# A recurrent mixer whose state step becomes one whole-array product, with its states kept and its output products in two batches

## The chip, the cores and the metric

The kernel runs on one core of a Trainium2 chip. The metric is the device time of one execution in microseconds (us). Three runs of the kernel before gave 2497.30, 2500.01 and 2503.43 us, so the median is 2500.01 us.

A core has engines that run side by side and wait for one another through semaphores: TensorE (PE; its weight loads are listed as PEld), VectorE (DVE), ScalarE (ACT), GpSimd (POOL) and SyncE (SP), which here only issues DMAs. PE writes into PSUM, eight banks of 128 partitions by 512 float32. All data here is float32. The trace records each float32 matmul as two MATMUL records with their weight loads, so its counts are twice those of the code.

## What is computed

One decoder layer over 1024 tokens of width 1024. Its first mixer, the one changed, is a recurrence with 16 heads of 64 channels:

```
S = S * w_t + (S a_t) b_t + v_t k_t        per head, S is 64 x 64
y_t = S r_t
y = (y - mean) / sqrt(var + eps) * w + b + bonus, then times a gate
```

The kernel does not step by token. It cuts the tokens into 16 chunks of 64, and for each chunk works out, by products that need no state, a transition E, an additive term L, a read-out matrix R and a local output Yl. What stays sequential is, for c = 0 to 15 and each head,

```
S(c+1) = E(c) S(c) + L(c)                  the chain
Y(c)   = S(c) R(c) + Yl(c)                 the outputs (each up to transposition)
```

## The kernel before

All work on this mixer is in phase_rwkv. Eight passes p = 0 to 7 (PAIRS) handle two heads each, head h on partitions 64h to 64h+63. Each engine has its own program in the code, written out by hand in the order of issue. In each pass PE makes the masked products of the chunks (grams) and transposes (turn), then the projections for pass p+1 (paired, project_v), then two stages chunks(p, g) with g = 0 and 1, of eight chunks each.

A stage on PE is, in order: X4 (level, for g = 0; for g = 1 it was made during the stage before), T4/N4 (L949, L952), X5 (L961), N5 (L972), UT (L986), ER (L994, which gives E and R), LY (L1008, which gives L and Yl), and then the chain of eight steps. Most of these are products of 64x64 matrices on quarters of the array. Each needs a VectorE or ScalarE result of the one before, and to hide that wait the code puts pieces of an unrelated projection between them: side(n) issues n products of 128x128 weights with 512 columns, and gap(p, g, i) is side(4). 28 such products make one unit of that projection, in the order M2, M1, M6, M7, M4, M5, M3. early(p, g) is true for g = 1 and p at most 5; such a stage holds 32 of them, the last four already of the next unit, the others 24 or 28.

A chain step on PE (L1016 to L1036) waits for the state, makes E(c) S(c) as one 64x64 product for each head (L1023), then the output product S(c) R(c), again one for each head (L1027), and in g = 0 on every second step four products of X4 for the next stage (L901). A side product follows on every second step, or on every step if early. VectorE adds L(c) to the result and writes the state into Sf, two buffers of 64 columns used in turn (L1682). After the last step VectorE adds Yl to all outputs of the stage into Y (L1691).

VectorE's stage (chunks at L1624) is also in a fixed order. For g = 1 it is: the mask of X4 (L1636), two steps of the generator beside (between(2), here the products at L1508 and L1512 for pass p+1), four sums of projection weights (side_sums, L1422 to L1430), and then the two additions into TN (L1643) for which PE's X5 waits. Later it fills ET with the decay on the diagonal (L1666) and adds E (L1672). GpSimd makes sums of projection weights and clears TN (L1373).

## Time and profile before

| | |
|---|---|
| median of three runs | 2500.01 us |
| span of the profiled execution | 2496.2 us |
| PE busy, share of the span | 2412.2 us, 97% |
| DVE busy | 1243.1 us, 50% |
| ACT busy | 570.2 us, 23% |
| POOL busy | 99.8 us, 4% |
| the eight passes lie at | about 145 to 1176 us |
| one pass lasts | about 129 us |

A time of a row is counted from the span's start. The start-to-start distance of two rows of PE is how long the engine was held by the first; the duration of a single matmul is longer, because matmuls are pipelined. An entry in brackets is the idle time of the engine ahead of the row and what ended it. PEclk is the clock that TensorE was granted, 1.00 for 2.4 GHz and 0.50 for 1.2 GHz.

### The profile page before, as it was taken

The numbers are of one execution on the slowest core, as the hardware profiler recorded it, in microseconds if no ns is written. First come the engines' busy times: TensorE is split into PE (matmuls) and PEld (weight loads), VectorE is DVE, ScalarE is ACT, GpSimd is POOL, SyncE is SP. The second block draws the span as 40 slices with busy tenths as digits, with TensorE's granted clock in tenths as the row PEclk, the third lists the DMA queues.
The fourth block names the chain that finished last, engine by engine and source line by source line (L and its number), as shares of the span: only waits on it lengthen the run. The fifth ranks groups of instructions, "written<-read, shape, count | busy, mean of one in ns | idle before, by whom it ended". The sixth has DMA issues, their size and how long they took to land. (4 is left out here: it accounts for less than half of the span.)

```text
span 2496.2 us, 39012 instructions
## 1 busy us (share of the span) xinstructions
PE 2412.2 (97%) x16519; PEld 1288.4 (52%) x16519; DVE 1243.1 (50%) x2080; ACT 570.2 (23%) x949; POOL 99.8 (4%) x97
## 2 busy tenths in 40 slices
PE   9999999999999999989999999999999999999996
PEld 5644557454565454744445976644455444443342
DVE  4646676767675858563585634465444411101103
ACT  3322323223232424121111354411100000000002
POOL 1000000000000000000000000000000100000002
PEclk9999999999999999999999999999999999999998
DMA  4111212121212121122434823163263999999997
GB/s 155 40 49 38 70 49 70 45 70 49 70 45 64 38 79 35 61 65 73 161 76 127 302 97 102 39 208 109 74 220 133 413 428 428 427 427 424 428 428 294
DMA packets 214908, 406.18 MB, mean 163 GB/s; under 512 B 64979, under 2 KB 166861, under 8 KB 202445
## 3 DMA queue, kind: packets, MB, share of 16 engines
q1 hardware_dynamic: 187152, 336.42, 36.9%
q10 hardware_dynamic: 22108, 47.32, 5.2%
q0 software_dynamic: 5472, 19.93, 2.1%
q8 instruction: 132, 2.16, 0.4%
q14 instruction: 44, 0.35, 0.0%
HBM read 329.07 MB, written 68.26 MB: 159 GB/s over the span
## 5 line engine op out<-in xcount | busy, mean ns | idle before, releaser
L3317 PE MATMUL moe_pp<-moe_ring,own_xT 128*128 128x512 f32 (+1 forms) x624 | 235.5, 599 | 1.4 <-DVE own_xT L3072 1.4
L3175 DVE COPY own_hidT<-moe_pp 128x512 f32<-128x512 f32 x22 | 15.2, 691 | 270.9 <-PE moe_pp L3326 270.9
L3317 PEld LDWEIGHTS moe_pp<-moe_ring,own_xT 128*128 128x128 f32 (+1 forms) x624 | 89.7, 167 | 107.0 <-issue 105.0
L742 PE MATMUL rwkv_pp<-mix_hT,rwkv_side_raw 128*128 128x512 f32 x240 | 116.7, 621 | 8.0 <-DMA rwkv_side_raw<-w_in 4.1
L3340 PE MATMUL moe_pp<-moe_ring,own_hidT 128*64 128x512 f32 (+1 forms) x368 | 120.1, 594 | 0.8 <-DVE own_hidT L3175 0.8
L2881 PE MATMUL moe_pp<-moe_ring,mix_hT 128*128 128x512 f32 x256 | 117.5, 610 | 3.3 <-DVEq L179 3.3
L671 PE MATMUL rwkv_pp<-mix_hT,rwkv_wt_kv 128*128 128x512 f32 x256 | 113.3, 595 | 0.0
L742 PE MATMUL rwkv_pp<-rwkv_TS,rwkv_side_sum 128*128 128x512 f32 x240 | 109.9, 601 | 2.8 <-ACT rwkv_TT L1259 1.7
L742 PE MATMUL rwkv_pp<-rwkv_TS,rwkv_side_raw 128*128 128x512 f32 x240 | 110.6, 603 | 0.8
L1682 DVE TENSOR_TENSOR rwkv_Sf<-rwkv_pp,rwkv_LY 128x64 f32<-128x64 f32 x128 | 28.7, 225 | 161.0 <-PE rwkv_pp L1023 161.0
L2309 PE MATMUL attn_pp<-att_yC,attn_wp 128*128 128x512 f32 x224 | 100.7, 597 | 0.0
L3436 ACT ACTIVATE own_yo<-moe_pp 128x1024 f32<-128x1024 f32 x22 | 22.5, 1024 | 324.7 <-PE moe_pp L3340 324.7
L1188 ACT ACTIVATE rwkv_side_zx<-rwkv_pp 128x512 f32<-128x512 f32 x40 | 23.9, 597 | 271.4 <-PE rwkv_pp L742 200.2
L3181 DVE TENSOR_TENSOR own_hid<-moe_pp,own_act_h 128x512 f32<-128x512 f32 x22 | 15.2, 692 | 139.1 <-PE moe_pp L3317 139.1
L3317 PE MATMUL moe_pp<-mix_yAB,own_xT 128*64 128x512 f32 (+1 forms) x240 | 80.5, 607 | 4.1 <-DMA moe_ring<-moe_w 3.8
L671 PEld LDWEIGHTS rwkv_pp<-mix_hT,rwkv_wt_kv 128*128 128x128 f32 x256 | 48.0, 190 | 63.9 <-issue 63.9
L1188 ACT ACTIVATE rwkv_side_ze<-rwkv_pp 128x512 f32<-128x512 f32 x40 | 23.9, 597 | 235.5 <-PE rwkv_pp L742 188.7
L2881 PEld LDWEIGHTS moe_pp<-moe_ring,mix_hT 128*128 128x128 f32 x256 | 48.1, 195 | 57.2 <-issue 57.2
L3340 PEld LDWEIGHTS moe_pp<-moe_ring,own_hidT 128*64 128x64 f32 (+1 forms) x368 | 43.2, 155 | 65.9 <-issue 65.9
L742 PEld LDWEIGHTS rwkv_pp<-rwkv_TS,rwkv_side_sum 128*128 128x128 f32 x240 | 43.9, 190 | 52.9 <-issue 47.4
L742 PEld LDWEIGHTS rwkv_pp<-mix_hT,rwkv_side_raw 128*128 128x128 f32 x240 | 43.6, 194 | 52.8 <-issue 42.2
L742 PEld LDWEIGHTS rwkv_pp<-rwkv_TS,rwkv_side_raw 128*128 128x128 f32 x240 | 43.4, 189 | 48.4 <-issue 45.0
(493 smaller groups left out, 4459.3 us busy)
## 6 DMA issues: line engine op xcount, KB each, us to landing
moe_ring<-moe_w SPq DMA_DIRECT2D x54, 2048.0 KB, 31.6
mix_yAB<-moe_w SPq DMA_DIRECT2D x18, 2048.0 KB, 32.4
mix_hT<-moe_w SPq DMA_DIRECT2D x17, 2048.0 KB, 31.7
rwkv_side_raw<-w_in SPq DMA_DIRECT2D x20, 1024.0 KB, 5.4
s_y<-mix_yAB SPq DMA_DIRECT2D x24, 512.0 KB, 11.8
moe_ring<-moe_w ACTq DMA_DIRECT2D x6, 2048.0 KB, 9.0
s_y<-own_yo ACTq DMA_DIRECT2D x22, 512.0 KB, 10.4
rwkv_wt_kv<-w_in SPq DMA_DIRECT2D x16, 512.0 KB, 4.4
```

The source lines that it names most:

```text
L671: mm = pe.matmul(pp[:, bank, :], w[:, kt, :], hT[:, kt, h * HALF:(h + 1) * HALF], start=kt == 0, stop=kt == KT - 1)
L742: mm = pe.matmul(pp[:, bank, :], left[:, part, :], right[:, part, :], start=fresh and part == 0, stop=part == HK - 1, skip_group_check=True)
L1188: act.activation(side_z[dst][:, :], pp[:, side_bank(u, name), :], ACT.Copy).then_inc(side_copied, 1)
L1682: dve.tensor_tensor(Sf[:, (c + 1) % 2, :], pp[:, 4, c2 * CH:(c2 + 1) * CH], LY[:, c2, 0, j, :], ALU.add).then_inc(PV["Sf"], 1)
L2309: mm = pe.matmul(pp[:, 4 + n % 4, :], wp[kt % 2][:, c, :] if kt else wp0[:, c, :], yC[:, c, h * HALF:(h + 1) * HALF], start=c == 0, stop=c ...
L2881: mm = pe.matmul(pp[:, 2 * (t % 2) + h, :], mT[:, kt, t * P:(t + 1) * P], wo[:, kt, h * HALF:(h + 1) * HALF], start=kt == 0, stop=kt == KT ...
L3175: dve.tensor_copy(hidT[:, :, :].rearrange("p k s -> p (k s)"), pp[:, 4, :]).then_inc(hidT_s, 1)
L3181: dve.tensor_tensor(hid[:, :], pp[:, 3, :], act_h[:, :], ALU.mult).then_inc(hid_s, 1)
L3317: mm = pe.matmul(pp[at, bank, :], xT[n % 2][:, kt, at], weights(w, n, h)[0][:, kt, :], start=kt == 0, stop=kt == KT - 1)
L3340: mm = pe.matmul(pp[at, 6 + c, :], hidT[:, j, at], weights("w2", n, h)[0][:, j, c * HALF:(c + 1) * HALF], start=j == 0, stop=j == FF // P - 1)
L3436: act.activation(yo[u][:, :], bank2(6), ACT.Copy).then_inc(copied, 1)
```

## The change

- The chain's product is one matmul of a 128x128 block-diagonal weight (ET, now 128 wide, head 0 in one corner, head 1 in the other) with the 64 state columns of both heads.
- States are no longer kept in Sf but in the columns of Y, all 16 of them. S(1) is a copy of L(0); S(16), which nobody reads, is not made. So seven products remain in each stage.
- The output products of all eight chunks are made in one batch, outputs(p, g), into PSUM bank 6. For g = 0 it stands in the next stage, behind gap(p, 1, 0) and ahead of T4/N4. For g = 1 it stands behind the chain. The addition into Y, output_sum, moves with it: for g = 0 it is now VectorE's second instruction in stage g = 1, ahead of between.
- X4 of stage g = 1 is made in one go behind LY, in bank 5.
- gap(p, g, 5) is left out where the stage is not early. Instead every step of the chain has a side product.
- GpSimd fills ET with its diagonal (128x1024, twice in a pass). VectorE adds E in two instructions, one for each half of the partitions.
- One constant and three small buffers go; the copy nb uses the buffer gb.

```diff
+        CHAIN, STATES = NCH - 2, NCH - 1
+        LEVEL_BANK = (0, 5)
+        Y_BANK = 6
...
-        ET = k.sb("ET", [P, 2, GJ, CH])
+        ET = k.sb("ET", [P, 2, GJ, P])
...
-        nb = k.sb("nb", [P, GRID, GRID])
+        nb = gb
...
+        def state(c):
+            return Y[:, c * CH:(c + 1) * CH]
...
             def gap(p, g, i):
-                if i or g or p + 1 == PAIRS:
+                if (i or g or p + 1 == PAIRS) and (i < 5 or early(p, g)):
                     side(4)
...
-                if jj == 0 and p:
-                    pe.wait_ge(PV["Y"], 2 * p)
...
+            def outputs(p, g):
+                n = 2 * p + g
+                pe.wait_ge(PV["RH"], n + 1)
+                pe.wait_ge(PV["S0"], p + 1)
+                pe.wait_ge(PV["Sf"], STATES * p + 8 * g + 7)
+                if n:
+                    pe.wait_ge(PV["Y"], n)
+                for i in range(2 * GJ):
+                    j, c2 = i // 2, i % 2
+                    for h in range(2):
+                        rows = slice(h * CH, (h + 1) * CH)
+                        mm = pe.matmul(pp[rows, Y_BANK, c2 * 256 + j * CH:c2 * 256 + (j + 1) * CH], state(8 * g + i)[rows], RH[rows, c2, j, :],
+                                       start=True, stop=True)
+                mm.then_inc(PM["Y"], 1)
...
                 gap(p, g, 0)
+                if g:
+                    outputs(p, 0)
                 pe.wait_ge(PV["Xf"], 5 * n + 1)
                 if n:
-                    pe.wait_ge(PV["Y"], n)
                     pe.wait_ge(PA["LY"], n)
...
                 mm.then_inc(PM["LY"], 1)
+                if g == 0:
+                    if p:
+                        pe.wait_ge(PV["Yg"], 2 * p)
+                    else:
+                        pe.wait_ge(PA["v"], 8)
+                    for m in range(GM, M):
+                        mm = level(1, m)
+                    mm.then_inc(PM["X4"], 1)
                 gap(p, g, 5)
-                pe.wait_ge(PV["RH"], n + 1)
-                pe.wait_ge(PA["LY"], n + 1)
...
+                pe.wait_ge(PV["E"], 2 * n + 2)
                 for i in range(2 * GJ):
                     c = 8 * g + i
                     j, c2 = i // 2, i % 2
-                    if i or g:
-                        pe.wait_ge(PV["Sf"], NCH * p + c)
-                    for h in range(2):
-                        rows = slice(h * CH, (h + 1) * CH)
-                        mm = pe.matmul(pp[rows, 4, c2 * CH:(c2 + 1) * CH], ET[rows, c2, j, :], Sf[rows, c % 2, :], start=True, stop=True)
-                    mm.then_inc(PM["S"], 1)
-                    for h in range(2):
-                        rows = slice(h * CH, (h + 1) * CH)
-                        mm = pe.matmul(pp[rows, 1, c2 * 256 + j * CH:c2 * 256 + (j + 1) * CH], Sf[rows, c % 2, :], RH[rows, c2, j, :],
-                                       start=True, stop=True)
...
-                    side(1 if early(p, g) or i % 2 else 0)
+                    if 0 < c < NCH - 1:
+                        pe.wait_ge(PV["Sf"], STATES * p + c)
+                        pe.matmul(pp[:, 4, c2 * CH:(c2 + 1) * CH], ET[:, c2, j, :], state(c), start=True, stop=True).then_inc(PM["S"], 1)
+                    if i == (0 if early(p, g) else 2):
+                        pe.wait_ge(PA["LY"], n + 1)
+                    side(1)
+                if g:
+                    outputs(p, 1)
...
+                for g in range(NG):
+                    if p or g:
+                        pool.wait_ge(PM["S"], CHAIN * p + 7 * g)
+                    pool.wait_ge(PV["pl"], p + 1)
...
+                    pool.tensor_tensor(ET[:, :, :, :], ident[:, :].unsqueeze(1).unsqueeze(1).to_broadcast([P, 2, GJ, P]), ends,
+                                       ALU.mult).then_inc(ends_set, 1)
...
+            def output_sum(p, g):
+                dve.wait_ge(PM["Y"], 2 * p + g + 1)
+                out = Y[:, g * HALF:(g + 1) * HALF].rearrange("p (j c t) -> p c j t", j=GJ, c=2)
+                dve.tensor_tensor(out, pp[:, Y_BANK, :].rearrange("p (c j t) -> p c j t", c=2, j=GJ), LY[:, :, 1, :, :],
+                                  ALU.add).then_inc(PV["Y"], 1)
...
-                dve.tensor_tensor(Xf[:, :, :], units(0), over(lfold[:, 0, :], GM), ALU.mult).then_inc(PV["Xf"], 1)
+                dve.tensor_tensor(Xf[:, :, :], units(LEVEL_BANK[g]), over(lfold[:, 0, :], GM), ALU.mult).then_inc(PV["Xf"], 1)
+                if g:
+                    output_sum(p, 0)
                 between(1 + g)
...
-                dve.tensor_tensor(ET[:, :, :, :], ET[:, :, :, :], both[:, :, :, 0, :], ALU.add).then_inc(PV["E"], 1)
+                for h in range(2):
+                    own = ET[rows_of(h), :, :, h * CH:(h + 1) * CH]
+                    dve.tensor_tensor(own, own, both[rows_of(h), :, :, 0, :], ALU.add).then_inc(PV["E"], 1)
...
+                    if c == 0:
+                        dve.tensor_copy(state(1), LY[:, 0, 0, 0, :]).then_inc(PV["Sf"], 1)
+                    elif c < NCH - 1:
+                        dve.wait_ge(PM["S"], CHAIN * p + c)
+                        dve.tensor_tensor(state(c + 1), pp[:, 4, c2 * CH:(c2 + 1) * CH], LY[:, c2, 0, j, :], ALU.add).then_inc(PV["Sf"], 1)
+                    if i == (1 if early(p, g) else 4):
+                        side_add(u, "F")
+                    if i == (3 if early(p, g) else 6):
+                        side_add(u, "C22")
+                if g:
+                    output_sum(p, 1)
```

## Rows read from the trace of the kernel before

**Rows 1.** Stretch, length, busy PE, PEld, DVE, ACT, POOL, PEclk, DMA share, GB/s.
```profile
200.00:1178.00 978.00, 952.62 (x10953) 525.93 (x10952) 642.26 (x1075) 280.55 (x406) 42.93 (x38) 1.00 0.20 58
```

**Rows 2.** PE's waits, 200 to 1180 us: total, times, longest.
```profile
PE rwkv_pp L1023 <- DVE rwkv_Sf L1682: 8.2, 40, 0.3
PE rwkv_pp L742 <- DMA rwkv_side_raw<-w_in: 4.1, 1, 4.1
...
PE rwkv_pp L986 <- DVE rwkv_Xf L1659: 1.1, 5, 0.2
```

**Rows 3.** Timeline of PE, pass 2, g = 1: start, duration, instructions merged.
```profile
522.48 3.70 PE L742 MATMUL rwkv_pp<-rwkv_TS,rwkv_side_sum 128*128 128x512 f32 x8
526.11 0.33 PE L1023 MATMUL rwkv_pp<-rwkv_Sf,rwkv_ET 64*64 64x64 f32 x4
...
526.49 1.12 PE L742 MATMUL rwkv_pp<-mix_hT,rwkv_side_sum 128*128 128x512 f32 x2
527.54 0.33 PE L1023 MATMUL rwkv_pp<-rwkv_Sf,rwkv_ET 64*64 64x64 f32 x4
...
537.58 0.45 PE L866 MATMUL rwkv_pp<-rwkv_RA,rwkv_icl 64*64 64x128 f32 x8
```

**Rows 4.** Timeline of PE, a run of side products.
```profile
1185.91 7.03 PE L742 MATMUL rwkv_pp<-rwkv_TS,rwkv_side_sum 128*128 128x512 f32 x16
1192.78 3.60 PE L742 MATMUL rwkv_pp<-rwkv_TS,rwkv_side_raw 128*128 128x512 f32 x8
```

**Rows 5.** Timeline of PE, pass 2, g = 0: side products before and behind the chain.
```profile
485.48 3.70 PE L742 MATMUL rwkv_pp<-rwkv_TS,rwkv_side_sum 128*128 128x512 f32 x8
...
497.46 3.60 PE L742 MATMUL rwkv_pp<-mix_hT,rwkv_side_raw 128*128 128x512 f32 x8
```

**Rows 6.** Timeline of PE, transposes in pass 0, 128x128 weights, 128 columns.
```profile
147.42 0.27 PE L888 MATMUL rwkv_pp<-main_ident,rwkv_sq 128*128 128x128 f32 x1
147.53 0.27 PE L888 MATMUL rwkv_pp<-main_ident,rwkv_v 128*128 128x128 f32 x1
```

**Rows 7.** Timeline of DVE, pass 2, a state addition in the chain.
```profile
527.92 0.22 DVE L1682 TENSOR_TENSOR rwkv_Sf<-rwkv_pp,rwkv_LY 128x64 f32<-128x64 f32 x1 [1.14 <-PE rwkv_pp L1023]
```

**Rows 8.** Timelines of PE and DVE, pass 0: X4 and its mask.
```profile
199.83 0.97 PE L901 MATMUL rwkv_pp<-rwkv_TN,rwkv_G 64*64 64x64 f32 x26
...
201.03 0.69 DVE L1636 TENSOR_TENSOR rwkv_Xf<-rwkv_pp,rwkv_lfold 128x512 f32<-128x512 f32 x1 [7.60 <-PE rwkv_pp L901]
```

**Rows 9.** Timelines of DVE and PE, pass 2, g = 1: up to X5.
```profile
498.26 0.68 DVE L1636 TENSOR_TENSOR rwkv_Xf<-rwkv_pp,rwkv_lfold 128x512 f32<-128x512 f32 x1
498.86 1.22 DVE L1508 TENSOR_TENSOR rwkv_kk<-rwkv_kk,rwkv_sq 128x1024 f32<-128x1024 f32 x1
...
503.78 1.28 DVE L1643 TENSOR_TENSOR rwkv_TN<-rwkv_TN,rwkv_pp 128x512 f32<-128x512 f32 x2
...
505.71 0.69 PE L961 MATMUL rwkv_pp<-rwkv_TN,rwkv_G 64*64 64x64 f32 x32
```

**Rows 10.** Timelines of PE and ACT, pass 7, g = 1: behind LY, and behind the chain.
```profile
1164.12 3.70 PE L742 MATMUL rwkv_pp<-rwkv_TS,rwkv_side_sum 128*128 128x512 f32 x8
1164.26 1.02 ACT L1280 ACTIVATE rwkv_LY<-rwkv_pp 128x1024 f32<-128x1024 f32 x1 [2.33 <-PE rwkv_pp L1008]
...
1176.09 1.90 PE L676 MATMUL rwkv_pp<-rwkv_lo,rwkv_lw 128*128 128x512 f32 x4
```

**Rows 11.** Timeline of DVE, pass 2, g = 0: E.
```profile
483.75 0.69 DVE L1672 TENSOR_TENSOR rwkv_ET<-rwkv_ET,rwkv_pp 128x512 f32<-128x512 f32 x1 [0.56 <-PE rwkv_pp L994]
```

**Rows 12.** Timelines of POOL, two sums in pass 0; of DVE, X4's mask in pass 2.
```profile
39.93 3.20 POOL L1358 TENSOR_TENSOR rwkv_TN<-rwkv_TN,rwkv_wt_kv 128x512 f32<-128x512 f32 x1
43.08 1.27 POOL L1359 TENSOR_TENSOR mix_wp<-rwkv_wt_kv,mix_wp 128x512 f32<-128x512 f32 x1
...
462.03 0.69 DVE L1636 TENSOR_TENSOR rwkv_Xf<-rwkv_pp,rwkv_lfold 128x512 f32<-128x512 f32 x1 [0.79 <-PE rwkv_pp L901]
```

**Rows 13.** Busy time and clock behind PE's longest wait (columns as in rows 1).
```profile
1097.00:1105.00 8.00, 6.75 (x27) 2.82 (x30) 6.25 (x8) 0.56 (x2) 0.00 (x0) 0.57 0.31 113
```

More of the change, by code:

```diff
@@ L141, in constants @@
     c["level_fold"] = (lm[:, :, :CH] + lm[:, :, CH:]).transpose(1, 0, 2).reshape(P, -1)
-    c["fold"] = (row % CH == col)[:, :CH]
     c["eye_block"] = np.tile(np.eye(GRID).reshape(1, -1), (P, 1))
@@ L566, in first_loads @@
             sp.dma_start(side_raw[:, :, :], weight_columns(w_in, 3 * A_WIDTH, 2 * P)).then_inc(lora_w_in, 16)
-            for dst, src in ((one_bd, cd["ones_bd"]), (below[:, :], cd["below"]), (fold, cd["fold"]),
-                             (lfold[:, :, :].rearrange("p l n -> p (l n)"), cd["level_fold"][:, 4 * CH:6 * CH]),
+            for dst, src in ((one_bd, cd["ones_bd"]), (below[:, :], cd["below"]),
+                             (spare_w[:, 1, :], cd["level_fold"][:, 4 * CH:6 * CH]),
                              (tb[:, :, :].rearrange("p a b -> p (a b)"), cd["eye_block"]),
@@ L766, in paired @@
                         pe.wait_ge(PV["bonus"], 2 * p)
+                    if p >= 2:
+                        pe.wait_ge(PV["Xf"], 5 * (2 * p - 3) + 1)
                     if p >= 3:
                         pe.wait_ge(PV["Yg"], 2 * p - 4)
+                if name == "M1" and p >= 2:
+                    pe.wait_ge(PV["Y"], 2 * p - 2)
                 if name == "M6":
@@ L900, in level @@
                 for c2 in range(2):
-                    mm = pe.matmul(units(0)[rows_of(1 - c2), m % GM, :], G[rows_of(c2), m, 0, :], inverse(c2, m), start=True, stop=True)
+                    mm = pe.matmul(units(LEVEL_BANK[g])[rows_of(1 - c2), m % GM, :], G[rows_of(c2), m, 0, :], inverse(c2, m),
+                                   start=True, stop=True)
                 return mm
@@ L917, in z0 @@
                 mm.then_inc(PM["Z0"], 1)
+            def outputs(p, g):
[10 more added lines that the diff above has]
+                        mm = pe.matmul(pp[rows, Y_BANK, c2 * 256 + j * CH:c2 * 256 + (j + 1) * CH], state(8 * g + i)[rows], RH[rows, c2, j, :],
+                                       start=True, stop=True)
+                mm.then_inc(PM["Y"], 1)
             def chunks(p, g):
@@ L1660, in chunks @@
                                           units(1 + r)[rows_of(r if upper else c2), xs, :], ALU.add).then_inc(PV["N5"], 1)
-                if n:
-                    dve.wait_ge(PM["S"], 8 * n)
-                    dve.wait_ge(PM["Y"], n)
-                ends = plast[p % 2][:, 8 * g:8 * g + 8].rearrange("p (j c) -> p c j", c=2).unsqueeze(3).to_broadcast([P, 2, GJ, CH])
-                dve.wait_ge(PV["pl"], p + 1)
-                dve.tensor_tensor(ET[:, :, :, :], fold.unsqueeze(1).unsqueeze(1).to_broadcast([P, 2, GJ, CH]), ends,
-                                  ALU.mult).then_inc(PV["diag"], 1)
                 between(1 + g)
                 dve.wait_ge(PM["ER"], n + 1)
-                dve.wait_ge(PV["diag"], n + 1)
+                dve.wait_ge(ends_set, n + 1)
                 both = pp[:, 0:2, :].rearrange("p c (j a n) -> p c j a n", j=GJ, a=2)
-                dve.tensor_tensor(ET[:, :, :, :], ET[:, :, :, :], both[:, :, :, 0, :], ALU.add).then_inc(PV["E"], 1)
+                for h in range(2):
+                    own = ET[rows_of(h), :, :, h * CH:(h + 1) * CH]
+                    dve.tensor_tensor(own, own, both[rows_of(h), :, :, 0, :], ALU.add).then_inc(PV["E"], 1)
                 toks = r_of(p)[:, g * HALF:(g + 1) * HALF].rearrange("p (j c t) -> p c j t", j=GJ, c=2)
+                if n:
+                    dve.wait_ge(PM["Y"], n)
                 dve.tensor_tensor(RH[:, :, :, :], both[:, :, :, 1, :], toks, ALU.add).then_inc(PV["RH"], 1)
                 if g == 0:
-                    dve.memset(Sf[:, 0, :], 0.0).then_inc(PV["S0"], 1)
+                    if p:
+                        dve.wait_ge(PV["Yb"], p)
+                        dve.wait_ge(PV["Yg"], 2 * p)
+                    dve.memset(state(0), 0.0).then_inc(PV["S0"], 1)
                 dve.wait_ge(PA["LY"], n + 1)
@@ L1680, in chunks @@
                     j, c2 = i // 2, i % 2
-                    dve.wait_ge(PM["S"], NCH * p + c + 1)
-                    dve.tensor_tensor(Sf[:, (c + 1) % 2, :], pp[:, 4, c2 * CH:(c2 + 1) * CH], LY[:, c2, 0, j, :],
-                                      ALU.add).then_inc(PV["Sf"], 1)
-                    if i in (1, 3):
-                        side_add(u, "F" if i == 1 else "C22")
-                dve.wait_ge(PM["Y"], n + 1)
-                if g == 0 and p:
-                    dve.wait_ge(PV["Yb"], p)
-                    dve.wait_ge(PV["Yg"], 2 * p)
-                out = Y[:, g * HALF:(g + 1) * HALF].rearrange("p (j c t) -> p c j t", j=GJ, c=2)
-                dve.tensor_tensor(out, pp[:, 1, :].rearrange("p (c j t) -> p c j t", c=2, j=GJ), LY[:, :, 1, :, :],
-                                  ALU.add).then_inc(PV["Y"], 1)
+                    if c == 0:
[9 more added lines that the diff above has]
+                    output_sum(p, 1)
                 side_add(u, "C12")
```

26 lines of the change are left out of this document (9 added, 17 removed).

## The prediction

> **What bounds the kernel now.** I read the busy times by stretch first. In the eight passes PE is busy 952.62 of 978 us and DVE 642.26, at a clock of 1.00 [rows 1]. Busy is not full use, though, so PE's waits come next: in the same stretch it waits 8.2 us for the state additions, 4.1 us once for a DMA and 1.1 us for Xf, and little else [rows 2]. So PE's order of issue is the path: what PE is spared shortens the pass one for one, and what makes PE wait lengthens it. The side products only help as cover, since their number does not change. Then I read the timeline of PE around two chains, and that of DVE around X5, as the place from which the change's own new wait can be priced.
>
> A side product holds PE for 0.86 us: eight of them (x16 records) start at 1185.91 and the next starts at 1192.78 [rows 4]. A step of the chain with one takes 527.54 - 526.11 = 1.43 us [rows 3], so a step has 0.57 us beside its side product. Of that, 0.38 us lies between the state product and the side product (526.11 to 526.49). The rest, about 0.2, is what it costs to go from 128x128 products back to 64x64 ones: the side product starts at 526.49, lasts 0.86, and the next state product starts at 527.54, not 527.35.
>
> **What the chain gains.** After the change a step is one 128x128 product of 64 columns and a side product, with no change of array shape. The trace has no such product. Its nearest row is a transpose, also with 128x128 weights, of 128 columns: 147.53 - 147.42 = 0.11 us a record [rows 6], 0.22 for the two records of a product. With half the columns it cannot stream in less than half of that, 0.11. I take 0.22, because the weights are as large as in that row and each is used once; the other end is 0.11. Above, a weight load could lie in the open at each step; the step then costs some 0.2 more, as at a change of shape now, so 0.42 is the upper end.
>
> The Trainium skill, "TensorE: Matmul & The Clock Gate", section on LDWEIGHTS, says that loading weights takes time by their columns and gives P / 1.2 ns, an estimate of 107 ns for 128 columns, whatever streams behind it. This speaks against a whole-array product of a block-diagonal matrix, half of whose weights are zeros. By that page a state product costs 0.21 us; by the streamed columns alone it would cost 0.11, and the kernel would be 12 us faster than I say. No row of this trace decides between the two.
>
> VectorE's part of a step fits: the state product starts at 527.54, the addition at 527.92, it lasts 0.22 [rows 7], and a dependent product can start at about 528.2, 0.7 us after the first. The new step is 0.86 + 0.22 = 1.08 us long, so the addition stays hidden. The two side additions of 0.68 us that VectorE makes between steps start behind a state addition and end before the next result, as now.
>
> Each stage has seven state products (1.54 us) and eight side products in its chain (6.86 us).
>
> Stage g = 0, all eight passes. Now, from the side products before the chain to those behind it, 497.46 - 485.48 = 11.98 us [rows 5], with eight side products. Afterwards: X4 in one go (32 records on two quarters; the same in stage g = 0 takes 0.93 us: 26 of them span 0.97 with their tail, x32 issue at 0.029 apiece [rows 8]), 6.86 and 1.54: 9.33 us. Gain 2.65 x 8 = 21.2 us.
>
> Stage g = 1, passes 0 to 5. Now 537.58 - 522.48 = 15.10 us, with twelve side products [rows 3]. Afterwards 3.43 for gap 5, 6.86, 1.54, a change of shape 0.20 and the 32 output records 0.93 (two quarters again, priced as X4): 12.96 us. Gain 2.14 x 6 = 12.8 us.
>
> Stage g = 1, passes 6 and 7, where gap 5 goes. Now 1176.09 - 1164.12 = 11.97 us in pass 7 [rows 10], and 0.2 more in pass 6, which changes shape behind it. Afterwards the second step needs LY, which ScalarE copies from 1164.26 for 1.02 us [rows 10]; with the addition and the semaphore PE can go on 1.50 us behind the start, where it arrives after 1.08, so it waits 0.42. Pass 6: 6.86 + 1.54 + 0.42 + 0.20 + 0.93 = 9.95, gain 2.2. In pass 7 PE must then wait for the addition into Y: in place of 0.93 stand 1.20 us from the first output record to VectorE's start (X4: 199.83 to 201.03 [rows 8]), 0.68 and 0.06, so 10.96, gain 1.0.
>
> Sum of the gains: 21.2 + 12.8 + 2.2 + 1.0 = 37.2 us.
>
> **What stage g = 1 loses.** output_sum(p, 0) is VectorE's second instruction in this stage, and it waits for outputs(p, 0), which PE issues behind gap 0. Queued behind it on VectorE are the two products of between, the four weight sums and the additions into TN, and for these PE's X5 waits. Count from the start T of gap 0 (497.46 [rows 5]). Now the additions into TN end at 503.78 + 1.28 = T + 7.60, and X5 starts at 505.71 = T + 8.25 [rows 9], by PE's own order. Afterwards gap 0 ends and the shape changes by T + 3.52, the result reaches VectorE 1.20 later, at T + 4.72, and the next VectorE instruction starts 0.60 behind that (as 498.26 to 498.86 [rows 9]), at T + 5.32. From there to the end of TN is 505.06 - 498.86 = 6.20 us, so X5 can start at T + 11.58. PE itself would be ready 0.93 later than now, at T + 9.18. It waits 2.40 us, and X5 is 3.33 us later than now. In pass 7 between is empty, so TN ends about T + 9.3 and X5 is only 1.2 us later. Sum: 3.33 x 7 + 1.2 = 24.5 us.
>
> Behind X5 the two engines stand to each other as now (PE waits at most 0.3 us for Xf [rows 2]), and nothing is given back: VectorE's later idle time cannot shorten PE's order.
>
> **What costs nothing.** E in two halves takes 0.68 us more: in g = 0 it starts at 483.75 [rows 11] and now ends at 485.1, still before LY ends on PE at 485.48. The mask at L1666 leaves VectorE. The added waits of PE (Yg, Y, Xf for bank 5 and 6) are for things done many microseconds before; if one were late, paired or X4 would wait. The longer turn at the end of a stage (Y, then C12) puts the first mask of the next pass 0.4 us later, with 2 us of PE work before anyone needs it. GpSimd's fills take about 2.5 us each (two times 1.27 [rows 12]). The first falls beside VectorE's mixing of keys. How the two engines hinder each other shows at the start: a GpSimd sum took 3.20 us beside a long VectorE addition, and 1.27 without [rows 12]. VectorE has 0.79 us in hand before X4's mask [rows 12]; a delay of 1.1 us would cost 0.3 in a pass. I take zero, up to 2 us in all.
>
> The Trainium skill, "GPSIMD Engine Reference", section on specifications, says that GpSimd shares its SBUF interfaces with VectorE and contends with instructions of two SBUF inputs. The slow sum agrees; by that page alone the 2 us would be spent.
>
> **Sum.** 37.2 gained and 24.5 lost: 12.7 us faster. From the profiled span of 2496.2 us that is 2483.5; the median of the runs is 3.8 us above the span, so I predict 2487.3 us. With the state product at 0.11 it would be 2475, at 0.42 it would be 2510 (112 products, 1.12 us for each 0.01).
>
> **Rivals.**
> - The stall is absent, since something that I don't see lets VectorE go ahead. Only the 0.93 us of outputs would be lost in eight stages, 7.4 us, and the time would be 2470. Against it stands VectorE's fixed order. 0.08.
> - Slower: the weights of each state product load in the open, because the product sits behind a wait. For it speaks that at every step now the load starts only with the product; against it, that this comes with a change of shape there. At 0.42 us the 112 products cost 22 more, 2510 us. It decides from 0.33 us on, where the gain is gone. 0.11.
> - The clock falls in the new waits. Behind the 4.1 us wait [rows 2] it fell to 1.2 GHz: its mean over 8 us is 0.57 [rows 13], so it stood at 0.50 for 0.43 x 8 / 0.5 = 6.9 us and lost half of that, 3.4 us. In seven stages that is 24: 2511 us. But the new wait is 2.4 us, and PE is busy up to it. 0.07.
> - The change does not do what it says for time: a step stays bound by something like the round trip through VectorE, or GpSimd holds VectorE up by more, and gain and loss cancel: within 5 us of 2500. 0.09.
> - The forecast as summed: 0.65, its own range 2477 to 2495.
>
> The range of 8 in 10 reaches to the first rival and over the cancelled gain: 2468 to 2504. A measurement of this kernel tells 0.3%, 7.5 us. Of the forecast's 0.65, 0.52 lies below 2492.5, the rest within 0.3%. Faster 0.52 + 0.08 = 0.60; same 0.13 + 0.09 = 0.22; slower 0.18.
>
> **What would show it.** In the changed trace the state products should stand 1.08 us apart in every stage, with no wait for the state. Right: PE idle about 2.4 us ahead of X5 in g = 1 of passes 0 to 6, released by VectorE's TN additions, and VectorE idle about 3.2 us ahead of its addition into Y. X4's start to LY's end unchanged in g = 0. Wrong: a step over 1.2 us (the load in the open), no idle time ahead of X5, or a clock below 1.00 behind it.

## The result, and the profile after

The changed kernel takes 2509.91 us (median of 10 runs, 2502.25 to 2514.28) against 2500.0 us before (10 runs, 2497.3 to 2505.18): a ratio of 1.0038, 95% interval 1.0028 to 1.0048. I had predicted 2487.3 us, in a range of 2468 to 2504. The profiled execution took 2509.33 us with a span of 2507.4, against 2496.2 before, so the two spans are 11.2 us apart.

The busy time over the eight passes, the same stretch and columns as [rows 1]:

```profile
200.00:1178.00 978.00, 936.50 (x10619) 540.07 (x10618) 646.75 (x1060) 279.31 (x403) 71.32 (x53) 0.99 0.20 58
```

PE is busy 16 us less than before [rows 1] and yet the passes end later: PE now has more idle time on its path. Which idle time it is stands in PE's waits from 200 to 1180 us of the changed kernel (columns as in [rows 2]):

```profile
PE rwkv_pp L986 <- DVE rwkv_TN L1678: 16.1, 7, 2.3
PE rwkv_pp L909 <- issue: 6.7, 2, 3.6
PE rwkv_pp L748 <- DMA rwkv_side_raw<-w_in: 4.0, 1, 4.0
...
PE rwkv_pp L1033 <- issue: 2.4, 2, 1.4
PE rwkv_pp L817 <- ACT rwkv_sq L1175: 2.1, 6, 0.3
```

The 8.2 us for the state additions [rows 2] are gone. The first line (X5 behind TN) was forecast. The two "issue" lines (X4 and LY) and the last one (L817, for a result of ScalarE that comes late, see the fill below) were not. "Issue" is idle time in which the engine waits for nothing that the profile shows.

PE's timeline of the chain, pass 2, g = 1, which answers to [rows 3]:

```profile
529.35 0.33 PE L1051 MATMUL rwkv_pp<-rwkv_Y,rwkv_ET 128*128 128x64 f32 x2
529.52 1.08 PE L748 MATMUL rwkv_pp<-mix_hT,rwkv_side_sum 128*128 128x512 f32 x2
530.43 0.33 PE L1051 MATMUL rwkv_pp<-rwkv_Y,rwkv_ET 128*128 128x64 f32 x2
530.60 1.08 PE L748 MATMUL rwkv_pp<-mix_hT,rwkv_side_sum 128*128 128x512 f32 x2
531.51 0.33 PE L1051 MATMUL rwkv_pp<-rwkv_Y,rwkv_ET 128*128 128x64 f32 x2
```

From one state product to the next it is 1.08 us, where it was 1.43. With 0.86 us for the side product the state product costs 0.22, the value I took. The chain is what the prediction said; the loss is elsewhere.

To find it I cut every stage into stretches by PE's starts, and summed them over the passes, from the profiled executions. The table is worked out from PE's timeline; its last column is what my sum says of the same stretch.

| stretch on PE | before | after | difference | forecast |
|---|---|---|---|---|
| LY to the gram products, g = 1, passes 0 to 6 | 118.7 | 102.7 | -16.1 | -15.0 |
| LY (g = 0) to T4 (g = 1) | 142.2 | 139.8 | -2.4 | -13.8 |
| T4 to X5, g = 1 | 38.1 | 56.1 | +18.0 | about +17 |
| X5 to UT, g = 1 | 72.9 | 77.7 | +4.7 | 0 |
| gram products to T4, g = 0, passes 0 to 6 | 382.0 | 385.9 | +3.9 | 0, up to 2 |

The forecast of row 2 is -21.2 with the outputs' 0.93 us in eight stages added back; that of row 3 is 2.40 x 7. LY of the last stage starts 8.5 us later than before, which the rows and 0.24 us ahead of the first pass make up. The last row leaves out pass 7, where the same stretch takes 50.75 us before and 50.81 after. So three things beyond my sum cost 11.4, 4.7 and 3.9 us.

**The second row: PE runs out of instructions.** PE's timeline in pass 3, g = 0, changed kernel; the bracket is the idle time before a line and its releaser:

```profile
613.58 1.10 PE L1019 MATMUL rwkv_pp<-rwkv_TT 64*64 64x128 f32 x32
614.51 2.04 PE L1033 MATMUL rwkv_pp<-rwkv_TT 64*64 64x64 f32 x128
616.38 1.10 PE L909 MATMUL rwkv_pp<-rwkv_TN,rwkv_G 64*64 64x64 f32 x31
621.06 0.22 PE L909 MATMUL rwkv_pp<-rwkv_TN,rwkv_G 64*64 64x64 f32 x1 [3.57 <-issue]
```

PE has issued 31 of the 32 X4 records and then stands for 3.57 us, although no wait of the program holds it. Busy time, clock and DMA load around it (columns as in [rows 1]):

```profile
614.00:616.00 2.00, 2.00 (x132) 2.00 (x125) 1.22 (x2) 0.29 (x1) 0.00 (x0) 1.00 0.53 102
616.00:618.00 2.00, 1.48 (x71) 1.34 (x61) 1.12 (x4) 1.02 (x1) 0.00 (x0) 1.00 1.04 361
618.00:620.00 2.00, 0.00 (x0) 0.00 (x0) 0.00 (x0) 0.00 (x0) 0.00 (x0) 1.00 0.56 201
620.00:622.00 2.00, 0.94 (x2) 0.50 (x2) 0.00 (x0) 0.00 (x0) 0.00 (x0) 0.78 0.00 0
622.00:624.00 2.00, 2.00 (x5) 1.10 (x4) 0.23 (x1) 0.00 (x0) 0.00 (x0) 0.50 0.04 8
```

The DMA engines are full (1.04, 361 GB/s) when PE stops, and the clock stands at 0.50 (1.2 GHz) behind the gap. What fills them up to 618 us is one SyncE transfer, the side load of the stage (q1). SyncE's timeline, and the DMA packets by queue, of the changed kernel from 618 to 619 us (packets, MB, share):

```profile
613.68 0.38 SPq L569 DMA_DIRECT2D rwkv_side_raw<-w_in  x1
```

```profile
q10 hardware_dynamic: 129, 0.25, 63.5%
q1 hardware_dynamic: 136, 0.12, 35.4%
q8 instruction: 1, 0.02, 6.2%
```

From 610 to 618 us no packet of kind "instruction" starts; the first one, of some 16 KB, starts at 618.6, when the load is nearly through. ER, LY and X4 are 192 short records in a row, at 0.015 to 0.03 us each. The number of such packets goes with the number of PE's records: 130 on q8 for 32462 records with their weight loads, 132 for 33038 before. That is some 250 records a packet, an estimate, since the profile doesn't say whose instructions a packet holds. With their weight loads the 192 records are 384, so by it such a burst can't go through on one packet. From LY to T4 the first stages of passes 1, 2, 4 and 6 take 15.7 to 16.0 us; passes 0, 3, 5 and 7 take 17.5, 21.2, 17.0 and 20.7. Against 15.8 each these four lose 13.1 us. The kernel before had lost 2.0 us here itself (18.58 and 18.36 us in passes 0 and 1, against the usual 17.47; 1.2 of it shows as waits for issue), and the difference, 11.1, is nearly the whole 11.4 that row 2 lacks. Of the 13.1 us 9.1 are the waits for issue themselves (two at X4, two in LY). Where they are long, in passes 3 and 7, the halved clock behind them adds to it.

**The fourth row: the clock.** Busy time of the changed kernel around X5 in pass 2, g = 1:

```profile
505.00:508.00 3.00, 0.66 (x10) 0.13 (x11) 2.97 (x6) 0.00 (x0) 0.00 (x0) 1.00 0.00 0
508.00:511.00 3.00, 3.00 (x35) 1.60 (x35) 2.69 (x7) 0.00 (x0) 0.00 (x0) 0.58 0.03 5
511.00:514.00 3.00, 3.00 (x18) 1.10 (x20) 3.00 (x5) 0.09 (x1) 0.00 (x0) 0.85 0.00 0
```

PE stands 2.34 us and then runs at 1.2 GHz for (0.42 x 3 + 0.15 x 3) / 0.5 = 3.4 us. This follows X5 in passes 0, 1, 2 and 6, and costs 1.2 to 1.4 us each.

**The fifth row: GpSimd beside VectorE.** Timelines of DVE and POOL of the changed kernel, pass 2:

```profile
448.90 2.70 DVE L1492 SCALAR_TENSOR_TENSOR rwkv_k<-rwkv_k,rwkv_omp,rwkv_LY 128x1023 f32<-128x1023 f32 x1
```

```profile
448.63 1.90 POOL L1399 TENSOR_TENSOR rwkv_ET<-main_ident,rwkv_plast 128x1024 f32<-128x1024 f32 x1
```

The same operation of the kernel before:

```profile
448.11 1.27 DVE L1465 SCALAR_TENSOR_TENSOR rwkv_k<-rwkv_k,rwkv_omp,rwkv_LY 128x1023 f32<-128x1023 f32 x1
```

The fill of the transitions takes VectorE's key mixing from 1.27 to 2.70 us, once in each pass, and gram products to T4 grows from 54.34 to 54.92. The two operations overlap for 1.63 us (448.90 to 450.53), and VectorE loses 1.43 of it.

The profile thus names four costs against the chain's gain: the stall at X5 with the clock behind it, the starved issue, and the fill. None of this shows yet that taking one away gives its time back.

### The profile page after: what moved, and what is told of

Its sections match the earlier page's. It is cut to its first block and busy times, and to the rows that moved or that the text cites. A ratio compares the mean times of both kernels' runs of the same rounds, so it can differ in the third digit from the quotient of the medians.

```text
span 2507.4 us, 38457 instructions
## 1 busy us (share of the span) xinstructions
PE 2403.8 (96%) x16231; PEld 1308.2 (52%) x16231; DVE 1252.6 (50%) x2072; ACT 569.7 (23%) x949; POOL 128.7 (5%) x113
## 3 DMA queue, kind: packets, MB, share of 16 engines
q8 instruction: 130, 2.13, 0.4%
## 5 line engine op out<-in xcount | busy, mean ns | idle before, releaser
L748 PE MATMUL rwkv_pp<-rwkv_TS,rwkv_side_sum 128*128 128x512 f32 x240 | 121.3, 634 | 1.9 <-ACT rwkv_TT L1279 1.7
L1720 DVE TENSOR_TENSOR rwkv_Y<-rwkv_pp,rwkv_LY 128x64 f32<-128x64 f32 x112 | 25.1, 224 | 105.4 <-PE rwkv_pp L1051 103.8
```

What stands on the lines that cost most here:

```text
L748: mm = pe.matmul(pp[:, bank, :], left[:, part, :], right[:, part, :], start=fresh and part == 0, stop=part == HK - 1, skip_group_check=True)
L1720: dve.tensor_tensor(state(c + 1), pp[:, 4, c2 * CH:(c2 + 1) * CH], LY[:, c2, 0, j, :], ALU.add).then_inc(PV["Sf"], 1)
```

## The experiments

**Out of the way of X5.** The outputs of g = 0 go back to the end of their own chain.

```diff
                 gap(p, g, 0)
-                if g:
-                    outputs(p, 0)
 ...
                     side(1)
-                if g:
-                    outputs(p, 1)
+                outputs(p, g)
```

VectorE's output_sum moves in the same way, from behind X4's mask to the end of the chain.

> The changed kernel with the products for the outputs, and VectorE's add into Y, back at the end of each stage's chain, so that nothing of them stands ahead of X5. Theory A (my sum, mis-sized in its losses): the batch put ahead of X5 costs 2.57 us x 7 in the stretch from T4 to X5 and 1.2 us x 4 of halved clock behind it; both go, and the first stage of a pass gets 0.93 us x 8 of outputs back. T4 to X5 is 4.7 us again in every pass, the wait of TensorE for VectorE's TN at X5 (16.1 us in 7) is gone, no granted clock of 0.5 follows, and the time is 2510 - 22.7 + 7.4 = 2495, within 5. Theory B (the whole-array chain is itself the loss, and X5's stall only sits where another would be): the stall moves to the next product that needs VectorE, and the time stays at 2506 to 2514.

Measured: 2491.82 us (2489.25 to 2493.45, 6 runs), before 2500.37; ratio 0.996, 0.9948 to 0.9972. T4 to X5 sums to 38.1 us and X5 to UT to 72.9, both as before the change; PE no longer waits at X5 for TN. The chain is the same whole-array chain, so theory B is out. The starved passes are still there (LY to T4 takes 21.7 us in pass 3 and 23.1 in pass 7).

**X4 behind the chain.** The block of X4 (32 records of the trace) moves from before gap 5 to behind the eight steps; the code is unchanged otherwise.

```diff
                 mm.then_inc(PM["LY"], 1)
-                if g == 0:
 ...
-                    for m in range(GM, M):
-                        mm = level(1, m)
-                    mm.then_inc(PM["X4"], 1)
                 gap(p, g, 5)
 ...
                 if g:
                     outputs(p, 1)
+                if g == 0:
 ...
+                    for m in range(GM, M):
+                        mm = level(1, m)
+                    mm.then_inc(PM["X4"], 1)
```

> The changed kernel with the 32 X4 products of the first stage moved from behind LY to behind the chain. Theory A (the 11.5 us that four first stages lose between LY and T4, passes 0, 3, 5 and 7, are a supply of instructions that runs dry after 192 short products in a row): the waits for issue at X4 and LY (6.7 and 2.4 us) are gone or under 1 us each, the first stages of those passes take about 15.8 us from LY to T4 like the others, and the time is 2510 - 11.5 = 2498, within 5. Theory B (supply runs dry wherever the instruction stream is fetched while the side load of 1 MB is under way, however long the burst is): the waits for issue move to the chain's or the later records with the same sum, some 9 us, and the time stays at 2506 to 2513.

Measured: 2502.99 us (2500.41 to 2508.23, 12 runs), ratio 1.001, 1.0002 to 1.0019: 6.9 us less than the changed kernel, where I had said 11.5. The issue wait at X4 is gone, that at LY remains (2.2 us). Passes 3 and 7 fall from 21.2 and 20.7 to 16.65, but passes 1, 2, 4 and 6 rise from 15.9 to 16.8, and pass 5, whose wait for issue lies in LY, from 17.0 to 18.4. PE's timeline of pass 3 shows part of the reason: without X4 in between, the first state product has to wait for state(1).

```profile
617.08 1.13 PE L748 MATMUL rwkv_pp<-rwkv_TS,rwkv_side_sum 128*128 128x512 f32 x2
618.52 0.43 PE L1043 MATMUL rwkv_pp<-rwkv_Y,rwkv_ET 128*128 128x64 f32 x2 [0.32 <-DVE rwkv_Y L1717]
```

From the first side product to this state product it is now 1.44 us, where 0.96 is usual (487.76 to 488.72 in pass 2 of the changed kernel). X4 had been cover for LY's copy, at no cost. Its new place costs 0.9 us in a stage: this 0.48, and small pieces of 0.05 to 0.11 us, most of them where the array changes shape around X4. The time agrees with theory A, though the wait in LY had to go by it as well, and against B speaks that the chain's records did not begin to starve. But this run tells nothing of the load's part.

**The fill out of VectorE's way.** GpSimd's g = 0 fill moves from behind the memsets of TN to behind the sums of pair weights; in pass 2 it then runs at 408.23 instead of 448.63. The operation stands in a helper fill(p, g) now, and what follows the memsets keeps the fill of g = 1 alone.

```diff
                     pair_weight_sums(p + 1)
+                if p:
+                    pool.wait_ge(PM["S"], CHAIN * p)
+                pool.wait_ge(PV["pl"], p + 1)
+                fill(p, 0)
 ...
+                pool.wait_ge(PM["S"], CHAIN * p + 7)
+                fill(p, 1)
```

> The changed kernel with GpSimd's fill of the block-diagonal transitions for the first stage moved right behind its sums of pair weights, so that it no longer runs beside VectorE's key mixing. Theory A (the fill takes VectorE's two-input operation from 1.27 to 2.70 us, and this sits on the path once in each pass): the key mixing is back at 1.3 us, the stretch from the gram products to T4 of the first stage is 54.3 us instead of 54.9, and the time is 2510 - 3.9 = 2506, within 3. Theory B (the longer operation is hidden, and the 0.6 us of a pass is of another cause): the operation shortens, the stretch stays at 54.9, and the time stays within 2 of 2510.

Measured: 2504.85 us (2500.72 to 2507.64, 11 runs), ratio 1.0017, 1.0008 to 1.0026: 5.1 us less than the changed kernel. VectorE's timeline of this kernel, pass 2:

```profile
447.51 1.27 DVE L1497 SCALAR_TENSOR_TENSOR rwkv_k<-rwkv_k,rwkv_omp,rwkv_LY 128x1023 f32<-128x1023 f32 x1
```

Gram products to T4 sums to 382.2 us in passes 0 to 6, 382.0 before the change, and the wait at L817 (2.1 us, 6 times) is gone. The cost is real and on the path.

**All three.**

> All three edits together: outputs at the end of each stage's chain, X4 behind the chain, the first fill earlier. Theory A (three separate costs that were not or not fully in my sum took the gain): the edits add, 2510 - 15.3 - 11.5 - 3.9 = 2479, within 7, that is 0.8% below the kernel before. Theory B (the gain of the new chain is itself small, and the costs stand in each other's place): 2490 or more.

Measured: 2480.03 us (2479.56 to 2484.57, 4 runs), ratio 0.9913, 0.9898 to 0.9927. The three edits alone gave 18.1, 6.9 and 5.1, in sum 30.1; together they give 29.9. The costs add.

**Only the load later.** One wait ahead of SyncE's side load of a first stage.

```diff
                 for g in range(NG):
+                    if g == 0:
+                        sp.wait_ge(PM["S"], (NCH - 2) * p + 1)
                     next_side(stage_unit(p, g) + 1)
```

> The changed kernel with one wait added on SyncE's queue: the side load (1 MB of w_in) that a first stage issues waits for the first chain product of that stage, some 11 us later than in the changed kernel, so that it no longer flies while the 192 short products behind UT are issued. Theory A (the transfer keeps the DMA engines from bringing instructions, and the burst of short products uses them up meanwhile): the waits for issue at X4 and LY of passes 3 and 7 are gone or under 1 us each, the first stages of all passes take 15.7 to 16.3 us from LY to T4, and the time is 2510 - 11.5 = 2498, within 5; the X4 edit gave 7 of it because it costs 0.9 us a stage of its own. Theory B (instructions run dry by the length of the burst alone, whatever else flies): the waits for issue stay where they are, with 6 us or more, and the time stays within 4 of 2510. Against A could also go that the load now lands too late for the next stage: then TensorE waits for side_raw and the time is above 2510.

Measured: 2497.44 us (2495.0 to 2502.24, 12 runs), ratio 0.9988, 0.998 to 0.9997: 12.5 us less than the changed kernel, from one wait that moves one transfer. PE's timeline of pass 3, g = 0, and SyncE's load:

```profile
611.98 2.04 PE L1035 MATMUL rwkv_pp<-rwkv_TT 64*64 64x64 f32 x128
613.85 1.10 PE L911 MATMUL rwkv_pp<-rwkv_TN,rwkv_G 64*64 64x64 f32 x31
616.07 0.21 PE L911 MATMUL rwkv_pp<-rwkv_TN,rwkv_G 64*64 64x64 f32 x1 [1.12 <-issue]
```

```profile
617.54 0.38 SPq L569 DMA_DIRECT2D rwkv_side_raw<-w_in  x1
```

The burst of 192 records is as long as it was, at the same place of the program, and the wait ahead of the same record falls from 3.57 to 1.12 us. In this kernel an instruction packet lands between 612 and 614 us, inside the burst (DMA packets of that stretch):

```profile
q10 hardware_dynamic: 144, 0.26, 35.5%
q8 instruction: 1, 0.02, 3.3%
```

Narrower stretches of this view put the packet's start at 613.5 us, 2.5 behind ER's first record (611.05), and in the changed kernel at 618.6, 5.0 behind it (613.58). Without the load beside it the packet comes 2.5 us earlier, and the wait is 2.45 us shorter; in both kernels PE goes on 1.5 us behind the packet's end (it takes 1.0). So theory A holds for the larger part: the burst alone does not starve PE for long, the burst beside the load does. The 2.7 us that are left (1.5 at X4, 1.2 at LY) occur without the load, and passes 0, 3, 5 and 7 still take 16.4 to 17.1 us from LY to T4, where I had said at most 16.3. In the traces the waits for issue at X4 and LY fell by 6.4 us, the whole stretch from LY to T4 of g = 0 by 9.6 (139.8 to 130.2), since passes 3 and 7 no longer run at the halved clock behind the wait, and X5 to UT by 1.5 (77.7 to 76.2). Another 1.6 us of this profiled execution lies elsewhere: in pass 7 the stretch from the gram products to T4 takes 49.2 us instead of 50.8. PE stands there 3.9 to 4.1 us for a side load in every kernel of this document, and the clock stays at 0.50 behind it for 3.4 us in this execution and 6.8 in that of the changed kernel.

**Only the addition later.** VectorE's output_sum(p, 0) goes from ahead of TN to behind it; TensorE's order is that of the changed kernel.

```diff
                 dve.tensor_tensor(Xf[:, :, :], units(LEVEL_BANK[g]), ...)
-                if g:
-                    output_sum(p, 0)
 ...
                     dve.tensor_tensor(TN[:, r, ms, :], TN[:, r, ms, :], units(1 + r), ALU.add).then_inc(PV["TN"], 1)
+                if g:
+                    output_sum(p, 0)
```

> The changed kernel with only VectorE's add of the first stage's outputs into Y moved, from ahead of its TN adds to behind them; TensorE's products for the outputs stay in their batch ahead of T4. Theory A (the 2.57 us of the stretch from T4 to X5 are VectorE's in-order queue: TN stands behind an add that waits for products which TensorE issues late; the 0.93 us of products are no part of it): T4 to X5 is 4.73 us, the wait at X5 (16.1 us in 7) is gone, no clock of 0.5 follows X5, and the time is 2510 - 18.0 - 4.7 = 2487, within 4, that is below the kernel with the outputs at the end of each chain (2492), since the first stage keeps its 0.5 us each. Theory B (the batch of products itself delays T4's evacuation, by the banks or by the shapes): T4 to X5 stays at 6 us or more and the time at 2500 or more.

Measured: 2488.69 us (2483.65 to 2491.36, 6 runs), ratio 0.9951, 0.9937 to 0.9966: 21.2 us less than the changed kernel. VectorE's timelines show the whole mechanism. The changed kernel, pass 2, g = 1:

```profile
497.10 0.68 DVE L1669 TENSOR_TENSOR rwkv_Xf<-rwkv_pp,mix_wp 128x512 f32<-128x512 f32 x1
501.01 0.69 DVE L1654 TENSOR_TENSOR rwkv_Y<-rwkv_pp,rwkv_LY 128x512 f32<-128x512 f32 x1 [3.23 <-PE rwkv_pp L939]
...
506.54 1.27 DVE L1678 TENSOR_TENSOR rwkv_TN<-rwkv_TN,rwkv_pp 128x512 f32<-128x512 f32 x2
```

and with the addition behind TN:

```profile
488.99 0.68 DVE L1669 TENSOR_TENSOR rwkv_Xf<-rwkv_pp,mix_wp 128x512 f32<-128x512 f32 x1
489.59 1.21 DVE L1535 TENSOR_TENSOR rwkv_kk<-rwkv_kk,rwkv_sq 128x1024 f32<-128x1024 f32 x1
...
494.51 1.28 DVE L1676 TENSOR_TENSOR rwkv_TN<-rwkv_TN,rwkv_pp 128x512 f32<-128x512 f32 x2
495.71 0.68 DVE L1654 TENSOR_TENSOR rwkv_Y<-rwkv_pp,rwkv_LY 128x512 f32<-128x512 f32 x1
```

The 3.23 us ahead of the addition go, and TN starts 5.5 us behind the mask instead of 9.4. T4 to X5 is 4.88 us in passes 0, 2, 3, 4, 5 and 7, not quite 4.73. X5 to UT sums to 72.9: with the wait, the clock of 0.50 behind it is gone as well. The place of the products costs 0.16 us a stage beyond their own time; the place of one addition cost 21 us.

**Quarters instead of the whole array.** The state product as two 64x64 products on the diagonal, everything else as in the changed kernel.

```diff
-                        pe.matmul(pp[:, 4, c2 * CH:(c2 + 1) * CH], ET[:, c2, j, :], state(c), start=True, stop=True).then_inc(PM["S"], 1)
+                        for h in range(2):
+                            rows = slice(h * CH, (h + 1) * CH)
+                            mm = pe.matmul(pp[rows, 4, c2 * CH:(c2 + 1) * CH], ET[rows, c2, j, rows], state(c)[rows], start=True, stop=True)
+                        mm.then_inc(PM["S"], 1)
```

> The changed kernel with each chain product made of two 64x64 products on the diagonal quarters of the same transition instead of one 128x128 product; what is computed is the same. Theory A (the whole-array product costs one product's passes, 0.22 us of the 1.08 us of a step, and quarters cost a second product or a change of shape against the whole-array side product beside it): the step is 1.08 to 1.35 us, and the time is 2510 to 2540 by 98 to 112 steps of up to 0.27 us. Theory B (two quarters that use different rows and columns run beside each other at the price of one, and the gain of the change comes from the transition being built beforehand, not from the whole array): the step stays at 1.08 us within 0.03 and the time within 3 of 2510.

Measured: 2532.78 us (2528.91 to 2541.95, 5 runs), ratio 1.0132, 1.0113 to 1.0151: 22.9 us more than the changed kernel. PE's timeline, pass 2, g = 1:

```profile
547.08 0.33 PE L1053 MATMUL rwkv_pp<-rwkv_Y,rwkv_ET 64*64 64x64 f32 x4
547.34 1.12 PE L748 MATMUL rwkv_pp<-mix_hT,rwkv_side_sum 128*128 128x512 f32 x2
548.39 0.33 PE L1053 MATMUL rwkv_pp<-rwkv_Y,rwkv_ET 64*64 64x64 f32 x4
```

A step is 1.31 us. This divides the 0.35 us that a step gained (1.43 to 1.08): 0.23 is the whole-array form, which spares a second product and the changes of shape around the side product, and 0.12 is that the output products left the chain. By this the whole-array product is worth 112 x 0.23 = 26 us, an estimate; the 22.9 measured are not purely this, since PE's waits for issue changed as well (12.1 us from 200 to 1180 us in the profiled execution, which took 2541.95 us, against 9.1). The batches of outputs are worth nothing by themselves, by the same estimate: eight times 0.12 is 0.96 us in a stage, and the batch costs 0.93 and, in places, a change of shape. No run had the batches without the whole-array chain in the kernel before.

**The addition, the fill, and X4.**

> Three edits together: VectorE's add of the first stage's outputs behind TN, GpSimd's first fill earlier, X4 behind the chain. Theory A (each cost is its own, and the products may stay ahead of T4): 2510 - 22.7 - 5 - 7 = 2475, within 5, below the 2480 of the three edits with the outputs at the end of each chain. Theory B (the place of the products matters as well): 2480 or more.

Measured: 2479.23 us (2477.33 to 2480.37, 4 runs), ratio 0.9915, 0.9901 to 0.993. It is no better than all three with the outputs at the end of each chain (2480.03); the 3 us between their two bases (2491.82 and 2488.69) come back only in part. Between my theories it is not decisive.

**The three edits that cost nothing.** The addition behind TN, the fill earlier, the load later, X4 where the change has it.

> The changed kernel with the three edits that take away a cost without adding one: VectorE's add of the first stage's outputs behind TN, GpSimd's first fill earlier, the first stage's side load behind the first chain product. Theory A (the four costs add up, and without them the change gives what its chain alone gives): 2510 - 21.2 - 5.0 - 12.5 = 2471, within 5, some 1.2% below the kernel before. Theory B (they stand in part in each other's place): 2476 or more.

Measured: 2474.9 us (2472.49 to 2475.86, 4 runs), before 2501.6; ratio 0.9888, 0.9874 to 0.9902. This is the fastest version, 1.1% below the kernel before and 35 us below the changed kernel. It lies at the upper end of theory A. The single edits had given 21.2, 5.1 and 12.5, so 3.8 us of the sum are missing. PE's waits of this kernel, 200 to 1180 us:

```profile
PE rwkv_pp L750 <- DMA rwkv_side_raw<-w_in: 4.1, 1, 4.1
...
PE rwkv_pp L1035 <- issue: 2.3, 3, 1.2
PE rwkv_pp L911 <- issue: 2.3, 2, 1.2
```

No wait for TN is left. 4.6 us of issue waits are, 1.9 more than with the load's edit alone. The other place is pass 7 again: gram products to T4 takes 52.6 us here, and 49.2 to 49.5 in the profiled executions of the three single edits. The wait for the side load there is the same 4.1 us, but the clock is at 0.50 for 6.8 us behind it and for 3.4 us some 34 us earlier, against 3.4 in all there. Why the packets and the clock meet the program differently in this kernel was not tested.

**The same wait in the kernel before.**

> The kernel before with the same one wait on SyncE's queue: the side load of a first stage waits for the first chain product of that stage. Theory A (running out of instructions beside this load is a cost that the change made: the kernel before has two waits for issue of 0.9 us and little else there): 2500 - 2, within 3, so that no more than 2 of the 12.5 us which the wait gave in the changed kernel belong to the kernel before as well. Theory B (the later load is worth something by itself, by less contention with VectorE or with other transfers): 2492 or less.

Measured: 2499.76 us (2497.3 to 2506.78, 12 runs), before 2501.6; ratio 0.9999, 0.9989 to 1.0009. The later load is worth nothing there: LY to T4 sums to 141.2 us against 142.2, and another wait grew (below). So the long starving beside this load came with the change, which put X4's 32 records behind LY's 128 where they had been spread over the chain. The short waits inside LY were there before it: 0.78 us in pass 0 and 0.94 in pass 6.

## Why the prediction was wrong

I had forecast 12.7 us less and measured 9.9 more. The gains and the stall at X5 were right; what failed are three terms that stood at nothing. X4's records behind LY were priced as if their instructions were always at hand, and that cost 11.4 us, half of the miss. The clock behind the stall (4.7 us) and GpSimd's fill (3.9) are the other two. Another 3.7 us lie behind the mixer, where the change touches nothing. The first alone does not turn the result: with the load moved and nothing else the kernel takes 2497.44 us, a ratio of 0.9988, which is still no change by my 0.3%.

- **A step of the chain** (0.22 us taken, 0.11 to 0.42 as bounds): right: the step is 1.08 us in 13 of the 16 stages and 1.12 in the other three, with single longer ones; two of the 112 products wait, 0.1 us each. The rival of the weight load in the open did not occur. The Trainium skill's "TensorE: Matmul & The Clock Gate", section on LDWEIGHTS, gives P / 1.2 ns for P columns of weights, an estimate of 107 ns for the 128 of a record; the 0.22 us for the two records of a product with 64 columns agree.
- **The gain in g = 1** (15.0 us for passes 0 to 6): 16.1 measured. Pass 6 gained 3.4, not 2.2. Behind LY it went from 12.3 to 10.1 us, which is the 2.2 of the sum; the rest is a wait for issue in LY that the kernel before had there (PE's timeline of it) and the changed kernel has not:

```profile
1041.41 0.27 PE L1008 MATMUL rwkv_pp<-rwkv_TT 64*64 64x64 f32 x2 [0.94 <-issue]
```

  So 1.2 us of this gain is luck, and the sum was right. Pass 7 gained 1.0 from LY to the next products, as summed.
- **The gain in g = 0** (21.2, less 7.4 for the outputs): the step that failed, 13.8 us forecast and 2.4 measured. Apart from the starved passes a stage takes 15.7 to 16.0 from LY, 1.7 us less than the usual 17.47 before, as summed. But I priced X4's 32 records behind LY at their 0.93 us alone, as if issue were free, and the move put 192 short records in a row beside a 1 MB transfer. It cost 11.4 us in this stretch. Moving that transfer by one wait gives back 9.6 of them in the trace, and 12.5 in the time.
- **The stall at X5** (3.33 x 7 + 1.2 = 24.5): right in mechanism and size. The wait measured 2.34 us in pass 2 against 2.40, 16.1 in all against 16.8, and VectorE's idle time ahead of the addition 3.23 against 3.2. What I had not asked is how cheaply it can go.
- **The clock behind the stall** (rival at 0.07, 24 us): half true. It fell in four of seven passes, for 3.4 us instead of 6.9, and cost 1.2 to 1.4 us each, 4.7 in all, where the forecast had none. I had taken the size from a wait of 4.1 us [rows 13] and had given "the wait is shorter" too much weight: here the shorter wait gave a shorter fall in four passes and none in three. Why the same wait does both, no run shows.
- **GpSimd's fill** (zero taken, 0 to 2 us as bound): mis-sized. A delay of 1.43 us (1.27 to 2.70) is more than the 1.1 that I counted, and the 0.79 us of [rows 12] covered all but 0.6 of it: 3.9 us in the trace, and 5.1 in the time when it goes. The row of the slowed GpSimd sum [rows 12] showed the collision from GpSimd's side only; VectorE's loss had to be guessed from it. The Trainium skill's "GPSIMD Engine Reference", section on specifications, which speaks of contention with instructions of two SBUF inputs, bears on exactly this operation, and the trace agrees: it has two, and took 2.70 us. By that page the upper bound of 2 us was the better value, and still too low.

The sum, up to LY of the last stage: the forecast's rows give -11.7; 11.4 for the starved issue, 4.7 for the clock and 3.9 for the fill make 20.0, and 1 us more stall against 1.1 us more gain in g = 1 cancel. That is +8.2, against +8.5 in the traces. Behind it the last stage gives 1.0 back, so 3.7 of the 11.2 us between the spans lie behind the mixer. (The medians are 9.9 us apart, since the changed kernel's median lies 2.5 us above its profiled span, and not 3.8.) Of these 3.2 are seen: a wait for issue in a later part that the change doesn't touch, of 2.8 us before and of this in the changed kernel (PE's waits from 1178 us on):

```profile
PE moe_pp L3444 <- issue: 6.0, 1, 6.0
```

It has 5.9 to 6.1 us in eight of the nine kernels built from the changed one. In the kernel before with the later load it has 5.3, and the 0.5 us that this edit gained up to LY of the last stage are lost there. This may be a refill of instructions at a bad time. The length of PE's program alone does not explain it, for that kernel has PE's program of before and yet the longer wait. No run tested it: it stays open.

## What to carry to other kernels

When a product batch moves, look for who reads it: on an in-order engine the reader belongs behind the work that others wait for, and here the place of one addition was worth 21 us, more than half of the 37 us that the change gained in its stages by my sum. Long runs of very short instructions need their own supply over DMA; a large transfer that starts beside such a run can starve it, and here delaying the transfer by one wait gave more (12.5 us) than breaking up the run (6.9). A helper engine's operation that ends up beside a critical two-input VectorE operation should be priced at the time for which the two overlap, not at zero: here VectorE lost 1.43 of 1.63 us.

## What the runs showed of the hardware

- Instructions arrive as packets of some 16 KB on a DMA queue of their own (q8), 130 in the whole program (2.13 MB). Beside a 1 MB load, which took the DMA engines with up to 361 GB/s, the packet for a run of 192 short matmul records started 5.0 us behind the run's first record, and PE stood 3.6 us. With the load elsewhere it started 2.5 us behind it, and the same run lost 1.1 us.
- After a wait of 2.3 us TensorE ran at 1.2 GHz for 3.4 us in some passes (0, 1, 2 and 6 in the changed kernel, 0, 1 and 4 in the one with X4 moved) and not at all in others, with the same wait ahead of it. Behind a wait of 3.9 to 4.1 us in pass 7 it was 3.4 us in some profiled executions and 6.8 in others.
- A whole-array fp32 product of 64 columns between whole-array side products costs 0.22 us; two 64x64 quarters in its place cost 0.45, of which 0.19 lies behind the side product (547.34 + 0.86 to 548.39), where the shape changes back.
- A GpSimd product of 1.9 us that started 0.27 us ahead of a VectorE operation of two SBUF inputs took that from 1.27 to 2.70 us and was itself not slowed: moved away to 408 us, it took 1.89.
